# A projection moved by one slot, table loads behind three copies, and sums taken with the copies, in a two-block transformer kernel on one Trainium2 core

## The chip, the cores and the metric

The kernel runs on one core of one Trainium2 chip (trn2). The metric is the device time of one execution in microseconds (us). The kernel before takes 1443.23 us (median of three runs, 1443.16 to 1444.81). Arithmetic is fp32; the large products are split into a rounded high part and a low part (fp32r), three matmuls for one.

## The reference, cut to what matters

Two blocks of two layers each, on 256 tokens of width 1024. The change touches the attention of the first block only. In each of its layers:

```python
h = rms_norm(x, ln1_gain[l]); proj = h @ w_in[l]
o_nsa = nsa_mixer(...)        # 6 heads, selected, window and compressed branches
o_mla = mla_mixer(...)        # 5 heads
o_ret = retention_mixer(...)  # 5 heads; per head: mean and variance over 64 columns, then
                              # (o - mu) * rsqrt(var + eps) * gain, times silu(gate)
x = x + concatenate([o_nsa, o_mla, o_ret]) @ w_out[l]
x = x + square(relu(rms_norm(x, ln2_gain[l]) @ w_up[l])) @ w_down[l]
```

The rotary tables (cos and sin of position times rate) are computed once, at the start of layer 0.

## The kernel before, in words

Every weight passes through a stream. SyncE loads tiles of 1 MB into a ring of four places (`load`, L782). A tile holds two units. ScalarE rounds a unit to its high half `wH` (`feed`, L1522, L1533) once the unit four before it has been used, VectorE subtracts to get the low half `wL` (`feed`, L1973, L1978), and TensorE takes units in order (`next_unit`, L855, which waits for `lo_ready`). Each `project` (L922) is eight chunks of three matmuls into one of four banks in PSUM. Banks are given in the order in which `order1` (L272) names the products; `open_acc` (L841) waits until the bank's last content is drained. So every engine's queue is an order written by hand, and they meet at semaphores.

**Start of layer 0.** TensorE projects cq0, cq1, ckv (units 0 to 2), sums squares (`ss1`), projects q0 (unit 3, in cq0's bank), ks and q1, with the rotation of q0 in the middle of ks and that of ks in the middle of q1 (L1303 to L1305), then `latent_squares` (L1163), which opens the bank that VectorE drains when it reads the rotation of q0 (L2128), then the tokens' projections tm00 and tm01. ScalarE, after four high halves, does `sines` (L1564: waits for VectorE's angles, one Sin over 128x512, signals `trig_ready`), `warm_root` (L1542: one element, so that the root's table is loaded again), copies cq0, cq1, ckv from PSUM (L1613), feeds units 4 to 6, takes the root of ss1 (L1513), and copies q0, ks and q1 (L1617) with a unit behind each. SyncE, after the fifth tile, waits for `trig_ready`, issues 16 small copies of the tables (L819), and only then the sixth tile's load. VectorE does the angles, unit 3's low half, units 4 to 6, the root's refinement, unit 7, waits for the first four table copies (L2269), scales the table (L2188) and rotates q0 and ks.

**Attention.** 17 heads run in 19 slots. In slot i TensorE does one projection of the list `FILL1`, the scores of head i, the transposes of the weights of head i-1 (`weights_transposed`, L1061, which waits for ScalarE's exponentials, L1572 and L1574), the values of head i-2 (`values`, L1069), and small products listed in `END1` (L237): ro0 to ro4 (retention outputs) in slots 13 to 15, mt0 and mt1 (transposes of the mixed output) in slot 16, mt2 in slot 17. The list has 16 names, so slot 16 has a head but no projection; tm31, the last, is in slot 15, beside head 15. In slot 17 TensorE also does 5 filler products (`kept_busy`, L967), and behind mt2 begins the output projection: `side_by_side` (L881) waits for the three units of wo0, wo1, wo2 (units 24 to 26), opens three banks, does two fillers, and then chunk by chunk for the three. Units 24 and 25 are split in slot 14; unit 26 takes the place of a unit of tm31. ScalarE splits it at the end of slot 15 (L1732) and VectorE in slot 16 (L2504), ahead of the low halves of mt0 and mt1 (`mixed_low`, L1987).

**Retention outputs.** ScalarE copies each from PSUM (L1694), 128x128 (two token tiles of 64 columns). VectorE sums them (`group_centred`, L2425), subtracts the mean, squares and sums (`group_squares`, L2432), in slots 15 to 17. It adds one to the gate's tanh and multiplies (`group_gate_open`, L2439) in slot 15 and multiplies by the gain (`group_gate`, L2443) in slot 17. `output` (L2295) scales a head's values and needs TensorE's values of that head.

Of the kernel before, what the change touches and what calls it, by code (L numbers as in the profile page):

```python
# [18 lines left out]
TT = S // P  # L19
# [209 lines left out]
    return out  # L229


FILL1 = ["tm10", "tm11", "q2", "kc", "kw", "vc", "kpe", "rqa", "rka", "rqb", "rkb", "r4", "tm20", "tm21", "tm30", "tm31"]
SLOTS1 = NH1 + 2
MID1 = {3: ["q2"], 4: ["kc"], 5: ["kw"], 7: ["kpe"], 8: ["rqa"], 9: ["rka", "mq0"], 10: ["rqb", "mq1"],
        11: ["rkb", "mq2"], 12: ["r4", "mq3"], 13: ["mq4"]}
# [225 lines left out]
def trn_kernel(nc, consts, vec1, vec2, once, pos, xin, stream, out):  # L461
    ctx = ExitStack()
    with ctx:
# [367 lines left out]
        def _(pe):  # L831
# [48 lines left out]

            def side_by_side(names, y):  # L881

                parts = [blocks(next_unit()) for _ in names]
                banks = [open_acc(n) for n in names]

                def chunk(c):

                    for (wh, wl), a in zip(parts, banks):
                        last = split_product(a[:, 0:S], (wh[:, c, :], wl[:, c, :]), y(c), c == 0, c == KC - 1)
                        if c == KC - 1:  # L890
                            last.then_inc(acc_full, 1)

                return chunk
# [543 lines left out]
        def _(act):  # L1437
# [153 lines left out]
            for L in range(LAYERS):  # L1591
# [14 lines left out]
                            cs = slice(n - 1, n + 1) if n < KC - 2 else slice(n, n + 1)  # L1606
                            act.activation(sq[:, cs, :], x[:, cs, :], ACT.Square).then_inc(sq_ready, 1)
                feed(SPLIT)
                if L == 0:
                    sines()  # L1610
                    warm_root()
                for i, u in enumerate(UNITS1[:SIDE]):
                    take(A1, u, L, raw[:, RAW1[u], :])  # L1613
                feed(SIDE + SPLIT)
                plain_root("ss1", L)
                for i, u in enumerate(("q0", "ks", "q1")):
                    take(A1, u, L, raw[:, RAW1[u], :])  # L1617
                    feed(SIDE + SPLIT + i + 1)
                    if i == 0:
                        for j, v in enumerate(UNITS1[:SIDE]):  # L1620
                            act.wait_ge(acc_drained[A1.bank(v)], A1.drained(v, L))
                            act.activation(latsq3[:, j, :], raw[:, RAW1[v], :], ACT.Square).then_inc(latsq, 1)
# [46 lines left out]
                def taken_after(i):  # L1669

                    for name in END1.get(i, []):
                        n = int(name[-1]) if name[-1].isdigit() else None
                        if name[:3] == "hid":
                            take(A1, name, L, quarters[name == "hidv"], n=P)
                        elif name[:2] == "hs":
                            a = full(A1, name, L)
                            act.activation(gel[:, 0, 30 * (name == "hsv"):30 * (name == "hsv") + 30]
                                           .rearrange("p (g n) -> p g n", g=2),
                                           a[:, 0:32].rearrange("p (g n) -> p g n", g=2)[:, :, 0:N_CMP], ACT.Copy)\
                                .then_inc(acc_drained[A1.bank(name)], 1)  # L1680
                        elif name[:2] == "mq":
                            take(A1, name, L, qm[:, n, :])
                        elif name[:2] == "mk":
                            a = full(A1, name, L)
                            for h in range(n, min(n + 2, MLA_HEADS)):
                                last = act.activation(km[0:64, h, :], a[64 * (h - n):64 * (h - n) + 64, 0:S], ACT.Copy)
                            last.then_inc(acc_drained[A1.bank(name)], 1)
                        elif name[:2] == "mv":
                            take(A1, name, L, vm[:, n, :], n=320)
                        elif name == "ct":  # L1690
                            take(A1, name, L, pcT[0:96, :], rows=slice(0, 96))
                        elif name[:2] == "ro":
                            a = full(A1, name, L)
                            act.activation(ro_(n), a[:, 0:2 * HD].rearrange("p (t d) -> p t d", t=TT), ACT.Copy)\  # L1694
                                .then_inc(acc_drained[A1.bank(name)], 1)
                        elif name[:2] == "mt":
                            mixed_high(n)

# [9 lines left out]
                for i in range(SLOTS1):  # L1708
                    if i < NH1 - 1:
                        feed(fed_by(i))  # L1710
                    if fill1(i):
                        taken(fill1(i))
                    if (L, i) == (0, 1):
                        act.wait_ge(late_in, 16 * 3)
                        act.activation(ada_t, cb2, ACT.Tanh, scale=0.5).then_inc(ctanh, 1)
                    if 1 <= i <= NH1:
                        transposed_copy(i - 1, NH1, 0, L)
                    if i in (NH1 - 2, NH1 - 1):
                        exponentials(i, NH1, 0, L)
                    taken_after(i)  # L1720
                    if i == 8:

                        act.wait_ge(ge, L * 2 + 1)
                        act.activation(gel[:, 1, 0:60], gel[:, 1, 0:60], ACT.Exp, scale=-2.0 * GELU_C).then_inc(ge, 1)
                    if i == 12:

                        act.wait_ge(csub, L + 1)
                        act.activation(pc[:], pc[:], ACT.Exp).then_inc(cexp, 1)
                    if i < NH1 - 2:
                        exponentials(i, NH1, 0, L)  # L1730
                    if i == NH1 - 2:
                        feed(24 + SIDE)  # L1732
                    if i == NH1:
                        warm_root()

                        act.wait_ge(gn_v, L * 2 + 2)
                        act.activation(gnst[:, 3, :], gnst[:, 2, :], ROOT).then_inc(gn_y, 1)
# [170 lines left out]
        def _(dve):  # L1908
# [248 lines left out]
            for L in range(LAYERS):  # L2157
# [263 lines left out]
                def group_centred(first, end):  # L2421

                    o, _, st = group_views(first, end)
                    dve.wait_ge(acc_drained[A1.bank(f"ro{end - 1}")], A1.drained(f"ro{end - 1}", L))
                    link(nc.vector.tensor_reduce(st(0), o, AX.X, ALU.add))  # L2425
                    link(TSC(st(1), st(0), 1.0 / HD, None, ALU.mult))
                    link(TTN(o, o, st(1).unsqueeze(3).to_broadcast([P, TT, end - first, HD]), ALU.subtract))

# [24 lines left out]
                for i in range(SLOTS1):  # L2453
# [21 lines left out]
                        group_centred(3, RET_HEADS)  # L2475
                    if i >= 2:
                        output(i - 2)
                    if i == 15:
                        group_gate_open()
                    if i == 5:  # L2480
                        take_normed("vc")
                    if i == 6:
# [17 lines left out]
                    if i == 14:  # L2500
                        add_compressed()
                        decay_scores(4)
                    if i == 16:
                        feed(24 + SIDE)  # L2504
                    if i == 17:
                        dve.wait_ge(o_drained, L * NH1 + (NH1 - 1) + 1)
                        dve.sem_inc(mla_ready, 1)
# [1 line left out]
                    for name in END1.get(i, []):  # L2509
                        if name[:2] == "mt":  # L2510
                            mixed_low(int(name[2]))
                    if i == 17:
                        group_gate()
                    if i == SLOTS1 - 1:
                        for c in range(IN_TURN, HEADS_DONE):
# [467 lines left out]
```

## Time and profile before

| | |
|---|---|
| median of three runs | 1443.23 us |
| the profiled execution | 1442.89 us, span 1441.1 us |
| TensorE matmuls busy | 1425.9 us, 99% |
| TensorE weight loads busy | 1357.9 us, 94% |
| VectorE busy | 1127.3 us, 78% |
| ScalarE busy | 812.7 us, 56% |
| granted TensorE clock | 1.0 of full speed |
| first block's layer 0, attention | about 12 to 149 us |
| the same of layer 1 | about 331 us later |

Spans and starts are counted from the first instruction; the execution's own time is a little longer than the span. PE is TensorE's matmul, DVE is VectorE, ACT is ScalarE, SPq is the queue of SyncE that issues DMAs. In a timeline a row is: start, duration, engine, line, operation, out<-in, count, and in brackets the idle time of the engine before it with what ended it.

### The profile page before, as it was taken

The numbers are of one execution on the slowest core, as the hardware profiler recorded it, in microseconds if no ns is written. First come the engines' busy times: TensorE is split into PE (matmuls) and PEld (weight loads), VectorE is DVE, ScalarE is ACT, GpSimd is POOL, SyncE is SP. The second block draws the span as 40 slices with busy tenths as digits, with TensorE's granted clock in tenths as the row PEclk, the third lists the DMA queues.
The fourth block names the chain that finished last, engine by engine and source line by source line (L and its number), as shares of the span: only waits on it lengthen the run. The fifth ranks groups of instructions, "written<-read, shape, count | busy, mean of one in ns | idle before, by whom it ended". The sixth has DMA issues, their size and how long they took to land.

```text
span 1441.1 us, 27501 instructions
## 1 busy us (share of the span) xinstructions
PE 1425.9 (99%) x11122; PEld 1357.9 (94%) x11122; DVE 1127.3 (78%) x2045; ACT 812.7 (56%) x1470; POOL 87.4 (6%) x108
## 2 busy tenths in 40 slices
PE   8999999999999999999999999999999999999999
PEld 8989999889989999989999999999899999999998
DVE  6888788896888788897897688777679857876654
ACT  6575677434575587544646456545465554664442
POOL 0000000000000000000150220000005103000000
PEclk9999999999999999999999999999999999999999
DMA  8433488985334379986455454676544445445451
GB/s 286 168 141 123 149 319 315 351 312 220 118 118 176 132 255 333 346 338 237 166 184 181 178 184 164 222 266 252 199 162 168 176 147 184 168 176 205 176 203 61
DMA packets 44445, 297.43 MB, mean 206 GB/s; under 512 B 6048, under 2 KB 7200, under 8 KB 8992
## 3 DMA queue, kind: packets, MB, share of 16 engines
q1 hardware_dynamic: 42880, 295.13, 56.3%
q8 instruction: 89, 1.46, 0.4%
q0 software_dynamic: 1024, 0.53, 0.2%
q14 instruction: 36, 0.29, 0.1%
q10 hardware_dynamic: 416, 0.02, 0.0%
HBM read 293.56 MB, written 1.05 MB: 204 GB/s over the span
## 4 chain that ended last, share of the span: by engine, by line
PE 82%; DVE 12%; ACT 4%; issue 2%; DMA 0%; SPq 0%; DVEq 0%; ACTq 0%
PE acc L864 19%; PE acc L866 18%; PE acc L865 18%; PE acc L870 12%; PE acc L871 6%; DVE wL L1978 5%; ACT wH L1533 2%; PE ps_t L1066 1%; PE ps_s L1053 1%; PE ps_s L1051 1%; PE acc L1156 1%; DVE region L2622 1%; DVE hL L1992 0%; DMA x<-xin 0%; DVE tcs L2619 0%
## 5 line engine op out<-in xcount | busy, mean ns | idle before, releaser
L1978 DVE TENSOR_TENSOR wL<-ring,wH 128x1024 fp32r<-128x1024 f32 x444 | 550.6, 1247 | 218.8 <-ACT wH L1533 210.5
L864 PE MATMUL acc<-hH,wH 128*128 128x256 f32 (+1 forms) x2016 | 577.3, 286 | 6.6 <-ACT region L1460 2.6
L1533 ACT ACTIVATE wH<-ring 128x1024 fp32r<-128x1024 f32 x444 | 464.4, 1052 | 197.2 <-PE acc L871 73.9
L866 PE MATMUL acc<-hH,wL 128*128 128x256 f32 (+1 forms) x2016 | 568.4, 282 | 0.0
L865 PE MATMUL acc<-hL,wH 128*128 128x256 f32 (+1 forms) x2016 | 566.5, 281 | 0.0
L864 PEld LDWEIGHTS acc<-hH,wH 128*128 128x128 f32 x2016 | 379.7, 188 | 13.3 <-issue 5.3
L865 PEld LDWEIGHTS acc<-hL,wH 128*128 128x128 f32 x2016 | 380.8, 189 | 2.0 <-issue 1.4
L866 PEld LDWEIGHTS acc<-hH,wL 128*128 128x128 f32 x2016 | 381.0, 189 | 0.0
L870 PE MATMUL acc<-aHL,wH 128*128 128x512 f32 x448 | 156.7, 394 | 0.0
L871 PE MATMUL acc<-aHL,wL 128*128 128x256 f32 x448 | 124.3, 282 | 0.0
L1968 DVE SCALAR_TENSOR_TENSOR ring<-ring,onc 128x1024 f32<-128x1024 f32 x96 | 117.0, 1219 | 0.0
L870 PE MATMUL acc<-a2HL,wH 128*128 128x512 f32 x308 | 107.3, 393 | 0.0
L870 PEld LDWEIGHTS acc<-aHL,wH 128*128 128x128 f32 x448 | 83.3, 188 | 18.3
L1460 ACT ACTIVATE region<-acc 128x256 f32<-128x256 f32 (+3 forms) x114 | 42.8, 379 | 82.2 <-PE acc L866 78.2
L871 PEld LDWEIGHTS acc<-aHL,wL 128*128 128x128 f32 x448 | 84.2, 188 | 1.2
L871 PE MATMUL acc<-a2HL,wL 128*128 128x256 f32 x308 | 84.8, 283 | 0.0
L870 PEld LDWEIGHTS acc<-a2HL,wH 128*128 128x128 f32 x308 | 57.0, 188 | 12.2
L871 PEld LDWEIGHTS acc<-a2HL,wL 128*128 128x128 f32 x308 | 57.9, 188 | 1.1
L864 PE MATMUL acc<-wH,hH 128*128 128x256 f32 (+1 forms) x192 | 56.4, 294 | 0.1
L865 PE MATMUL acc<-wL,hH 128*128 128x256 f32 (+1 forms) x192 | 53.8, 280 | 0.0
L866 PE MATMUL acc<-wH,hL 128*128 128x256 f32 (+1 forms) x192 | 53.7, 280 | 0.0
L2817 POOL DMA_DIRECT2D weights<-region x32 | 16.8, 531 | 559.1 <-DVE region L2612 559.1
(398 smaller groups left out, 2274.3 us busy)
## 6 DMA issues: line engine op xcount, KB each, us to landing
ring<-stream SPq DMA_DIRECT2D x275, 1024.0 KB, 4.9
cst<-consts SPq DMA_DIRECT2D x1, 1363.0 KB, 14.9
x<-xin SPq DMA_DIRECT2D x4, 256.0 KB, 5.3
ring<-stream SPq DMA_DIRECT2D x2, 512.0 KB, 6.7
out<-x SPq DMA_DIRECT2D x3, 256.0 KB, 5.9
onc<-once SPq DMA_DIRECT2D x1, 516.0 KB, 15.5
weights<-region POOLq DMA_DIRECT2D x32, 16.0 KB, 1.8
v1all<-vec SPq DMA_DIRECT2D x1, 355.0 KB, 8.8
```

The costliest lines, as they stand in the source:

```text
L864: pe.matmul(out, w[0], y[0], start=first, stop=False)
L865: pe.matmul(out, w[0], y[1], start=False, stop=False)
L866: return pe.matmul(out, w[1], y[0], start=False, stop=last)
L870: high = lambda stop: pe.matmul(a[:, :], w[0], both, start=first, stop=stop)
L871: low = lambda: pe.matmul(a[:, 0:S], w[1], both[:, 0:S], start=False, stop=False)
L1051: pe.matmul(b[:, 0:P], q[:, 0:P], k[:, 0:P], start=True, stop=True)
L1053: pe.matmul(b[:, P:3 * P], q[:, P:S], k, start=True, stop=True).then_inc(s_full, 1)
L1460: act.activation(dst, a[rows, 0:n], func, **kw).then_inc(acc_drained[tn.bank(name)], 1)
L1533: act.activation(wH[:, n % SPLIT, :], ring[:, g % RING, half * UNIT:(half + 1) * UNIT], ACT.Copy)\
L1968: STT(products, products, 1.0, cb2, ALU.mult, ALU.mult, accum_out=adac[:, L, 2 * j + half:2 * j + half + 1])\
L1978: TTN(wL[:, n % SPLIT, :], ring[:, g % RING, half * UNIT:(half + 1) * UNIT], wH[:, n % SPLIT, :].bitcast(F32), ALU.subtract).then_inc(lo_r ...
L2817: pool.dma_start(swapped[b % 2][to:to + 8], qk2[row:row + 8, 2 * b:2 * b + 2, :]).then_inc(swapped_in[b % 2], 16)
```

## The change

Six edits, all in the first block's attention:

- `FILL1` gets an empty place ahead of tm31, so tm31 is projected in slot 16 and slot 15 has no projection. The order of the products and their banks follow from it: ro4 comes ahead of tm31.
- `side_by_side` waits for each unit right before its first chunk, not for all three ahead.
- At the start of layer 0 ScalarE's `sines` and `warm_root` stand behind the copies of cq0, cq1, ckv, units 4 to 6 and the root of ss1.
- ScalarE copies a retention output as two instructions of 64 columns, each with its sum (`accum_out`), and VectorE's reduction is left out.
- Unit 26 is split by ScalarE at the end of slot 16 and by VectorE in slot 17, behind mt2's low half.
- `group_gate_open` moves on VectorE from slot 15 to slot 17, behind unit 26.

```diff
-FILL1 = ["tm10", "tm11", "q2", ..., "tm20", "tm21", "tm30", "tm31"]
+FILL1 = ["tm10", "tm11", "q2", ..., "tm20", "tm21", "tm30", None, "tm31"]
...
             def side_by_side(names, y):
 
-                parts = [blocks(next_unit()) for _ in names]
+                parts = []
                 banks = [open_acc(n) for n in names]
 
                 def chunk(c):
 
-                    for (wh, wl), a in zip(parts, banks):
+                    for i, a in enumerate(banks):
+                        if c == 0:
+                            parts.append(blocks(next_unit()))
+                        wh, wl = parts[i]
...
                 feed(SPLIT)
-                if L == 0:
-                    sines()
-                    warm_root()
                 for i, u in enumerate(UNITS1[:SIDE]):
                     take(A1, u, L, raw[:, RAW1[u], :])
                 feed(SIDE + SPLIT)
                 plain_root("ss1", L)
+                if L == 0:
+                    sines()
+                    warm_root()
                 for i, u in enumerate(("q0", "ks", "q1")):
...
                         elif name[:2] == "ro":
                             a = full(A1, name, L)
-                            act.activation(ro_(n), a[:, 0:2 * HD].rearrange("p (t d) -> p t d", t=TT), ACT.Copy)\
-                                .then_inc(acc_drained[A1.bank(name)], 1)
+                            for t in range(TT):
+                                at = t * RET_HEADS + n
+                                last = act.activation(ro_(n)[:, t, :], a[:, HD * t:HD * t + HD], ACT.Copy,
+                                                      accum_out=gnst[:, 0, at:at + 1])
+                            last.then_inc(acc_drained[A1.bank(name)], 1)
...
-                    if i == NH1 - 2:
-                        feed(24 + SIDE)
+                    if i >= NH1 - 2:
+                        feed(24 + min(i - NH1 + 4, SIDE))
...
                     dve.wait_ge(acc_drained[A1.bank(f"ro{end - 1}")], A1.drained(f"ro{end - 1}", L))
-                    link(nc.vector.tensor_reduce(st(0), o, AX.X, ALU.add))
...
-                    if i == 15:
-                        group_gate_open()
...
-                    if i == 16:
-                        feed(24 + SIDE)
...
                     for name in END1.get(i, []):
                         if name[:2] == "mt":
                             mixed_low(int(name[2]))
+                    if i == 16:
+                        feed(24 + 2)
                     if i == 17:
+                        feed(24 + SIDE)
+                        group_gate_open()
                         group_gate()
```

## Rows read from the trace of the kernel before

**Rows 1.** The page, its first part: busy time, share of the span, instructions.
```profile
PE 1425.9 (99%) x11122; PEld 1357.9 (94%) x11122; DVE 1127.3 (78%) x2045; ACT 812.7 (56%) x1470; POOL 87.4 (6%) x108
```

**Rows 2.** Waits of TensorE, whole run: us in total, times, longest us.
```profile
PE ps_s L970 <- DVE mtL L1987: 1.2, 2, 0.6
```

**Rows 3.** Timeline of ScalarE, start of layer 0.
```profile
21.58 0.63 ACT L1567 ACTIVATE region<-region 128x512 f32<-128x512 f32 x1 [4.04 <-DVE region L1955]
22.23 1.28 ACT L1544 ACT_TABLE_LOAD   x1
...
23.76 0.94 ACT L1460 ACTIVATE region<-acc 128x256 f32<-128x256 f32 x3
24.57 2.96 ACT L1533 ACTIVATE wH<-ring 128x1024 fp32r<-128x1024 f32 x3
...
27.68 0.40 ACT L1460 ACTIVATE region<-acc 128x256 f32<-128x256 f32 x1
...
42.29 2.00 ACT L1533 ACTIVATE wH<-ring 128x1024 fp32r<-128x1024 f32 x2
```

**Rows 4.** Timeline of VectorE, start of layer 0.
```profile
21.58 1.23 DVE L1978 TENSOR_TENSOR wL<-ring,wH 128x1024 fp32r<-128x1024 f32 x1
...
32.59 0.68 DVE L2188 TENSOR_TENSOR trig<-trig,rn 128x512 f32<-128x512 f32 x1
...
33.65 0.42 DVE L2128 TENSOR_TENSOR tss<-acc,trig 128x256 f32<-128x256 f32 x1
```

**Rows 5.** Timeline of TensorE, start of layer 0.
```profile
20.67 0.38 PE L977 MATMUL acc<-weights,one 128*128 128x256 f32 x1
...
24.29 0.36 PE L864 MATMUL acc<-hH,wH 128*128 128x256 f32 x1 [2.59 <-ACT region L1460]
...
28.63 0.38 PE L1035 MATMUL acc<-region,cst 128*128 128x256 f32 x1
...
34.21 0.45 PE L1163 MATMUL acc<-weights,one 128*128 128x256 f32 x1 [0.28 <-DVE tss L2128]
```

**Rows 6.** SyncE's table copies; a load at 33.4 to 33.6, and small transfers (us to landing).
```profile
22.30 11.13 SPq L819 DMA_DIRECT2D trig<-region  x16
...
ring<-stream SPq DMA_DIRECT2D x1, 1024.0 KB, 4.8
...
weights<-region POOLq DMA_DIRECT2D x32, 16.0 KB, 1.8
```

**Rows 7.** Timeline of ScalarE, end of slot 14 of layer 0.
```profile
127.22 0.28 ACT L1694 ACTIVATE region<-acc 128x128 f32<-128x128 f32 x1 [0.39 <-PE acc L1252]
127.39 0.39 ACT L1572 ACTIVATE weights<-weights,nmax 128x128 f32<-128x128 f32 x1
...
128.18 0.19 ACT L1574 ACTIVATION_READ_ACCUMULATOR weights<-weights,nmax 128x1 f32 x1
```

**Rows 8.** Timeline of TensorE, slot 15 of layer 0.
```profile
127.96 0.34 PE L864 MATMUL acc<-wH,hH 128*128 128x146 f32 x1
...
130.70 0.43 PE L1051 MATMUL ps_s<-region 96*128 96x128 f32 x2
...
131.40 0.39 PE L1066 MATMUL ps_t<-cst,weights 128*128 128x128 f32 x2
```

**Rows 9.** Timeline of TensorE, slot 17 of layer 0.
```profile
136.95 0.39 PE L1076 MATMUL ps_o<-region,weights 128*128 128x64 f32 x2
...
138.17 0.68 PE L970 MATMUL ps_s<-one 128*128 128x128 f32 x4 [0.61 <-DVE mtL L1987]
...
139.40 0.28 PE L864 MATMUL acc<-mtH,wH 128*128 128x256 f32 x1
```

**Rows 10.** Timeline of VectorE, slots 16 and 17 of layer 0.
```profile
136.14 1.22 DVE L1978 TENSOR_TENSOR wL<-ring,wH 128x1024 fp32r<-128x1024 f32 x1
...
138.13 0.29 DVE L2305 TENSOR_TENSOR region<-ps_o,coef 128x128 f32<-128x128 f32 x1
...
139.56 0.42 DVE L1987 TENSOR_TENSOR mtL<-acc,mtH 128x256 fp32r<-128x256 f32 x1
```

More of the change, by code:

```diff
@@ L229, in down_steps @@
     return out
-FILL1 = ["tm10", "tm11", "q2", "kc", "kw", "vc", "kpe", "rqa", "rka", "rqb", "rkb", "r4", "tm20", "tm21", "tm30", "tm31"]
+FILL1 = ["tm10", "tm11", "q2", "kc", "kw", "vc", "kpe", "rqa", "rka", "rqb", "rkb", "r4", "tm20", "tm21", "tm30", None, "tm31"]
 SLOTS1 = NH1 + 2
```

## The prediction

> **What bounds the kernel.** I read the page first: TensorE is busy for 1425.9 of 1441.1 us [rows 1], so only what stands in TensorE's way counts, and a change that takes nothing away from TensorE can give back its idle time and no more. Then the waits: the changed places hold one wait of 2.59 us at the start [rows 5] and one of 0.6 us at the end of the attention, twice, once a layer [rows 2]. The rest was read engine by engine in the timeline round those two places. The kernel has an order written by hand in each queue, so each part is followed as "who is ready when", in times of the old trace.
>
> **Part 1, the start (layer 0 only).** Before: ScalarE loads the sine's table, idles 4.04 us until VectorE has the angles, does the sine at 21.58, loads the root's table at 22.23, and only then copies cq0, cq1, ckv, from 23.76 [rows 3]. TensorE is done with the sum of squares by 21.5 and wants cq0's bank for q0; it starts at 24.29 [rows 5]. The change puts the three copies first. They no longer hold q0, but q0 needs its own low half, whose subtraction VectorE starts at 21.58 and ends at 22.81 [rows 4], and nothing in VectorE's order changes. So q0 starts at 22.86, 1.43 us earlier, not 2.59.
> What is late next: the transform of q0 in the middle of ks needs ScalarE's copy of q0, which now stands behind the sine. ckv's last product runs just ahead of the sum of squares at 20.67 [rows 5], so its copy starts at about 20.85 and the next instruction at 21.14. Three units and the root of ss1 take 27.68 - 24.57 = 3.11 us [rows 3]: 24.25. Then the first table load, hidden in those idle 4.04 us before and on the path now, 1.28; the sine to the next load 22.23 - 21.58 = 0.65; second load and warm-up 23.76 - 22.23 = 1.53 [rows 3]. The copy of q0 starts at 27.71, where it started at 27.68 before. From such a copy to TensorE's next instruction it was 24.29 - 23.76 = 0.53, so the transform comes at 28.24 instead of 28.63 [rows 5]: TensorE reaches it at 27.2 and waits 1 us. Of 1.43 there remain **0.39 us**.
> The chip needs no longer for a table than the row shows. The Trainium skill, "ScalarE: Activation LUTs", section "What ACT_TABLE_LOAD costs", wants more: 1283 ns for the load and some 1380 ns of drain, 2.66 us for every switch. Its 1283 ns stand in the trace, the drain does not; what the sum would be by it is a rival below.
> The next wait of TensorE is 0.28 us at 34.21, for VectorE's reading of the transform of q0, which began at 33.65 [rows 4, 5]. It needs the first table's copies. Their condition, the sine's end, moves from 22.21 to 24.25 + 1.28 + 0.63 = 26.16. SyncE issues 16 of them in 11.13 us, 0.7 each [rows 6], so the fourth is out at 28.95 and, at 1.8 us to landing for 16 KB [rows 6], there at 30.8. VectorE, whose root and unit 7 come over 2 us earlier, starts the scaling then instead of at 32.59 [rows 4], and the 0.28 us go too. Start: **-0.67 us**; bounds, from the two rows just used: -1.71 (no new wait) and +0.5 (the copies land 3 us later than so).
> Queued behind those copies on SyncE are the loads of weights. The next left at 33.4 and now leaves at 26.25 + 11.13 = 37.4; at 4.8 us [rows 6] its tile is there at 42.2. ScalarE began to split it at 42.29 in the old trace [rows 3], behind tm01. So nothing is lost, with half a microsecond of room: a rival.
>
> **Part 2, tm31 one slot later, and the unit of wo2.** No instruction of TensorE goes or comes; both layers alike. Before: in slot 17 TensorE waits until 138.17, as wo2's bank waits for mt1's low half, and VectorE makes that behind unit 26's low half, begun at 136.14 [rows 9, 10]. The wait costs its 0.61 of idle time and 0.16 more, since two matmuls that take 0.28 each start 0.11 apart (two in 0.39) [rows 9]: 0.77. After: VectorE makes mt0's and mt1's low halves first, at slot 16, so the banks are free; wo0 and wo1 take their first chunk while unit 26 is still open. So far that is a gain.
> But unit 26 now stands in VectorE's slot 17, behind output(15), three instructions of squares and mt2's low half. output(15) needs TensorE's values(15), whose last pair ends at 136.95 + 0.39 = 137.34 [rows 9]. From the start of output(15)'s product at 138.13 to mt2's low half it is 139.56 - 138.13 = 1.43, then 0.42, then the unit's 1.22 [rows 10]: 3.07, and with some 0.08 for two semaphores, wo2's first product can start 3.15 us after values(15). In the old trace it started at 139.40 [rows 9], 2.06 after. Nothing else for TensorE lies between: mt2, two fillers and the two chunks of wo0 and wo1 end about 1.9 us too early. So the old wait goes and a longer one takes its place: **+1.09 us a layer**. Bounds: +0.3, if half of the squares overlapped the wait, and +1.3, if unit 26's high half is late too.
> ScalarE makes that high half after slot 16's exponentials (tm31 must be done first) by about 137.5, before VectorE asks; it delays the copy of head 16's weights to 137.9, which TensorE wants only after 142. group_gate_open (0.8 us, as its like) now stands behind unit 26 as well: VectorE has then the two gate products and a reciprocal, under 2 us, while TensorE does 0.4 + 1.1 + 0.6 us until output(16) can read. It is covered; were the cover gone it would cost its 0.8. Everything behind follows one to one: TensorE waits for VectorE there as before, and is the bound again after it.
>
> **Part 3, slot 15 without a projection.** tm31 ran from 127.96 to 130.70 between the scores and the weights of head 14. The transposes of head 14 now follow the scores of head 15 directly: at 127.96 + (131.40 - 130.70) = 128.66 [rows 8]. Head 14's exponentials end at 128.18 + 0.19 = 128.37 [rows 7]: just in time.
>
> **Part 4, sums with the copies.** VectorE loses a reduction of some 0.5 us in slots 15 and 16. It then waits for TensorE anyway: worth nothing. ScalarE pays: a copy of 128 columns lets the next one start after 127.39 - 127.22 = 0.17 [rows 7]. Two copies of 64 columns with a sum each are not in the trace. Lower bound: nothing more. Upper: an accumulating exponential of 128 columns holds the engine for all of its 0.39, so two such, less 0.17, are +0.6. I take +0.28, nearest the copy's own duration (0.28) less a little, twice. ro2's lies in idle time; ro3's is right ahead of head 14's exponentials: 128.65, and at about 0.25 from ScalarE to TensorE 128.9 against 128.66. **+0.24 us a layer**, 0 to 0.55.
>
> **Sum.** 2 x (1.09 + 0.24) - 0.67 = +2.0 us. The profiled execution took 1442.89 us, 0.34 under the median of 1443.23; so 1444.9 against its own time, and 1445.2 as a median. A measurement of this kernel can tell about 0.2%, 2.9 us, from no change: the forecast is inside.
>
> **Rivals.**
> The wait goes and none takes its place (0.15). For it: the waits named in rows 2 and 5 are the two that the edit addresses. Against: VectorE's order. Price: 2 x 0.77 and 0.67 to 1.71 at the start, -2.2 to -3.2: 1440.0 to 1441.0. It decides if unit 26's low half ends before TensorE has done wo0 and wo1, 1.4 us after values(15).
> Balance (0.16): the start keeps its 1.43, or the squares are hidden; +1.09 a layer shrinks to 0.3 to 0.8. About 1443.2, within 1.
> Slower: the weights behind the tables (0.08). Against it: nothing but the last copies shares the queue with this load, as before, when it took 4.8 us [rows 6]. Landing after 42.8, TensorE waits as long as it is later, as slot 0's scores stand behind these two units on VectorE; it decides at 43.6, from where the total passes 1446.1. At 45.5: 1447.9.
> Slower still by the drain (0.01): twice 1.38 more ahead of q0's copy, the transform at 31.0, 1448.3. Against it speaks the old trace: from the second load to the copy of cq0 it is 1.53 in all [rows 3], with the load's 1.28 and a warm-up in it. That is the rule of the page named above; by the row, it is out.
>
> **Chances.** Forecast 0.60, its own range 1442.5 to 1446.8. Slower by over 0.2% (above 1446.1): 0.13 of the forecast's, and the last two rivals, 0.22. Faster (below 1440.3): 0.12, of the first rival 0.09, and the forecast's far tail. The rest, 0.66, is within. The range from 1440.5 to 1447.3 leaves out the last two rivals and half of the first.
>
> **What would show it.** At the start q0 at 22.9, TensorE waiting about 1 us in ks for ScalarE, the table copies from 26.2 and the next load at 37.4. In the tail the wait before the fillers gone, and a wait of about 1.9 us before the third product of wo's first chunk, by VectorE's subtraction of weights, in both layers; no such wait, or one under 0.8, makes the forecast wrong. ScalarE's retention copies x20 with reads of the accumulator, and a short wait before head 14's transposes.

## The result, and the profile after

| | before | changed |
|---|---|---|
| median | 1443.24 us, 14 runs | 1445.61 us, 14 runs |
| lowest to highest | 1443.07 to 1444.81 | 1443.74 to 1449.30 |
| profiled execution, span | 1442.89, 1441.1 us | 1445.42, 1443.6 us |
| granted clock, mean | 1.000 | 0.999 |

The ratio is 1.0017, with a 95% interval from 1.0010 to 1.0024: slower by 2.4 us, within the 0.2% that count as no change, and 0.4 us from the forecast of 1445.2. Before anything is explained, look at the spread: 5.6 us against 1.7. (Part of that is chance: three larger sets of runs of the kernel before, below, spread over 3.4 to 3.7 us, and a second set of the changed kernel over 4.0.) And the mean clock has lost 0.001.

Part 1 of the page of the changed kernel, against [rows 1]: TensorE is busy for 1.5 us more, though no instruction of it came or went. VectorE is busy for 3.5 us less, of which the four reductions that are gone (0.41 to 0.55 us each) make 1.9, and ScalarE for 1.3 more, with 30 more instructions.

```profile
PE 1427.4 (99%) x11122; PEld 1359.1 (94%) x11122; DVE 1123.8 (78%) x2041; ACT 814.0 (56%) x1500; POOL 87.3 (6%) x108
```

TensorE's waits in the changed kernel (us in total, times, the longest):

```profile
PE acc L864 <- DVE wL L1984: 6.1, 7, 1.8
PE acc L1038 <- ACT region L1463: 0.9, 1, 0.9
```

The wait ahead of the fillers [rows 2] is not in the list any more. The first row read 1.8 in 5 waits before. New in it are the waits for VectorE's low half of weights at q0 (1.2) and at wo2 in each layer (1.8). The second row is the new wait in ks.

**The start.** TensorE's timeline of the changed kernel:

```profile
22.19 0.39 PE L864 MATMUL acc<-hH,wH 128*128 128x256 f32 x1 [1.18 <-DVE wL L1984]
...
27.61 0.70 PE L1038 MATMUL acc<-region,cst 128*128 128x256 f32 x2 [0.89 <-ACT region L1463]
...
32.86 0.60 PE L1166 MATMUL acc<-weights,one 128*128 128x256 f32 x2
```

Its first product of all came 0.69 us sooner than in the execution before (11.04 against 11.73), as its first weights had landed sooner; in another execution of the kernel before it starts at 12.00, so this is no part of the change. Taken off, q0 is 2.10 - 0.69 = 1.41 us earlier than in [rows 5], and latent_squares 1.35 - 0.69 = 0.66.

A better mark than the first product is the start of VectorE's low half of unit 3. It comes right behind the angles that the sine waits for. So in both kernels it moves with what q0 waits for, the copies behind the sine before and that low half now:

```profile
20.91 4.63 DVE L1984 TENSOR_TENSOR wL<-ring,wH 128x1024 fp32r<-128x1024 f32 x4
```

From its start q0 took 24.29 - 21.58 = 2.71 us [rows 4, 5] and takes 22.19 - 20.91 = 1.28; latent_squares took 12.63 and takes 11.95. That is 1.43 and 0.68 us sooner, and it repeats within 0.01 in all five traces that have the sine behind the root. The mark itself lies anywhere from 20.86 to 22.21 us in the fourteen traces, whatever the kernel: this alone moves an execution by up to 1.35 us.

The queue that decides between the two is ScalarE's:

```profile
23.31 0.37 ACT L1516 ACTIVATE rn<-acc 128x256 f32<-128x256 f32 x1
23.70 1.28 ACT L1570 ACT_TABLE_LOAD   x1
25.00 0.63 ACT L1570 ACTIVATE region<-region 128x512 f32<-128x512 f32 x1
25.65 1.28 ACT L1547 ACT_TABLE_LOAD   x1
26.94 0.20 ACT L1547 ACTIVATE warm<-one 128x1 f32<-128x1 f32 x1
27.18 0.38 ACT L1463 ACTIVATE region<-acc 128x256 f32<-128x256 f32 x1
```

The sine and its tables take 27.18 - 23.70 = 3.48 us, all of it between the root and the copy of q0 that TensorE waits for. Each load is followed by the next instruction within 0.02 us: no drain stands behind it.

**The tail.** TensorE and VectorE of the changed kernel, slots 16 and 17 of layer 0, against [rows 9, 10]:

```profile
135.74 0.61 PE L973 MATMUL ps_s<-one 128*128 128x128 f32 x4
136.11 0.36 PE L864 MATMUL acc<-mtH,wH 128*128 128x256 f32 x1
...
138.82 0.39 PE L864 MATMUL acc<-mtH,wH 128*128 128x256 f32 x1 [1.76 <-DVE wL L1984]
```

```profile
135.79 0.29 DVE L2311 TENSOR_TENSOR region<-ps_o,coef 128x128 f32<-128x128 f32 x1 [0.62 <-PE ps_o L1079]
136.23 0.42 DVE L2437 TENSOR_TENSOR region<-region 128x256 f32<-128x256 f32 x1
136.69 0.42 DVE L2438 TENSOR_REDUCE region<-region 128x4 f32<-128x256 f32 x1
137.14 0.17 DVE L2439 TENSOR_SCALAR region<-region 128x4 f32<-128x4 f32 x1
137.22 0.42 DVE L1993 TENSOR_TENSOR mtL<-acc,mtH 128x256 fp32r<-128x256 f32 x1
137.55 1.22 DVE L1984 TENSOR_TENSOR wL<-ring,wH 128x1024 fp32r<-128x1024 f32 x1
```

VectorE's rows are the queue that the prediction walked: output(15), three instructions of squares, mt2's low half, and only then unit 26. wo2's first product waits for its end. From the last product before to it TensorE loses 138.82 - 136.78 - 0.11 = 1.93 us (136.78 is the start of that product, 0.11 the usual spacing); in layer 1 it is 1.94. Where the execution had stood 1.66 us ahead of the one before, it stands 0.58 ahead: +1.08, and +1.06 in layer 1.

**The clock.** Windows of the changed kernel around wo's first chunk in layer 1 (us, then busy time of PE, PEld, DVE, ACT, POOL, each with its count; then granted clock, DMA share, GB/s):

```profile
470.00:472.80 2.80, 1.03 (x9) 0.85 (x8) 2.73 (x6) 1.17 (x3) 0.00 (x0) 1.00 0.00 0
472.80:476.30 3.50, 3.50 (x20) 3.50 (x19) 1.20 (x4) 0.42 (x2) 0.00 (x0) 0.51 0.02 5
476.30:480.00 3.70, 3.70 (x32) 3.53 (x32) 2.87 (x7) 1.37 (x3) 0.00 (x0) 1.00 0.00 0
```

TensorE waits 1.94 us, runs from 471.95, and at 472.8 its granted clock drops to half, 1.2 in place of 2.4 GHz, for 3.41 us. In 3.5 us it does 20 matmuls; the kernel before does 33 in the same window:

```profile
472.80:476.30 3.50, 3.50 (x33) 3.50 (x32) 2.74 (x8) 1.61 (x3) 0.00 (x0) 1.00 0.00 0
```

The execution's lag behind the one before grows by 1.5 us there. Nothing in the prediction speaks of it.

The bridge of the two spans, from starts of the same matmuls: inputs -0.7, start -0.7, slot 0 -0.3, tail +1.1, behind it +0.1, two small steps of +0.2 and +0.4 near 263 and 288 us, tail of layer 1 +1.1, clock +1.5, the rest -0.1: +2.5, as 1443.6 - 1441.1. The 0.3 of slot 0 is a gain that the prediction did not name: in the kernel before, TensorE's transposes of head 0 start at 48.65, 0.32 us behind the product ahead of them in place of 0.12, and 0.25 behind the end of ScalarE's exponentials. In the changed kernel nothing holds them.

### The profile page after: what moved, and what is told of

The parts are those of the page before. It is cut to its first block, busy times and chain, and to the rows that moved or that the text cites. A ratio compares the mean times of both kernels' runs of the same rounds, so it can differ in the third digit from the quotient of the medians.

```text
span 1443.6 us, 27525 instructions
## 1 busy us (share of the span) xinstructions
PE 1427.4 (99%) x11122; PEld 1359.1 (94%) x11122; DVE 1123.8 (78%) x2041; ACT 814.0 (56%) x1500; POOL 87.3 (6%) x108
## 3 DMA queue, kind: packets, MB, share of 16 engines
HBM read 293.56 MB, written 1.05 MB: 204 GB/s over the span
## 4 chain that ended last, share of the span: by engine, by line
PE 76%; DVE 14%; ACT 5%; DMA 3%; issue 1%; DVEq 0%; POOL 0%; ACTq 0%; POOLq 0%
PE acc L864 17%; PE acc L866 17%; PE acc L865 17%; PE acc L870 11%; DVE wL L1984 6%; PE acc L871 6%; DMA ring<-stream 3%; ACT wH L1536 2%; DVE ring L1974 1%; PE ps_t L1069 1%; PE ps_s L1056 1%; PE ps_s L1054 1%; PE ps_t L973 1%; PE acc L1159 1%; PE ps_o L1079 1%
## 5 line engine op out<-in xcount | busy, mean ns | idle before, releaser
L870 PE MATMUL acc<-aHL,wH 128*128 128x512 f32 x448 | 156.9, 394 | 0.1
L870 PE MATMUL acc<-a2HL,wH 128*128 128x512 f32 x308 | 107.3, 393 | 0.0
L870 PEld LDWEIGHTS acc<-aHL,wH 128*128 128x128 f32 x448 | 83.3, 188 | 18.9 <-DVE wL L1984 0.7
L870 PEld LDWEIGHTS acc<-a2HL,wH 128*128 128x128 f32 x308 | 57.0, 188 | 12.2
```

Source lines behind the costliest of these rows:

```text
L870: high = lambda stop: pe.matmul(a[:, :], w[0], both, start=first, stop=stop)
```

## The experiments

All were compared with runs of the kernel before on the same chip, whose medians were 1443.22 (25 runs), 1443.20 (33) and 1443.33 (27) in the three batches. Line numbers shift by a few between kernels.

### The change taken apart

**The kernel before once more**, for its trace.

> The kernel before, once more, for a second trace of it. Both theories: 1443.1 to 1443.6 us, clock at its upper level all the way. It shows how far the first inputs' landing (7.67 us for the first weights in the old trace, 7.22 in the changed kernel's) moves by itself: if that is chance, a start between 11.0 and 11.8 us for the first product is seen here too.

1443.46 us. Windows around the start's wait:

```profile
20.00:24.40 4.40, 1.98 (x14) 1.55 (x13) 2.46 (x5) 2.97 (x7) 0.00 (x0) 1.00 0.98 399
24.40:28.00 3.60, 3.60 (x20) 3.60 (x19) 2.47 (x3) 3.19 (x5) 0.00 (x0) 0.53 0.90 310
```

The kernel before loses its clock too, here after the start's wait: I had expected full clock all the way, a miss. The first trace of it had not lost it (31 matmuls in the window where this has 20). Whether it happens thus changes from execution to execution. As one fall of 3.41 us takes 0.0012 off the mean clock, every run's mean clock tells about how many it had: 1.000 none, 0.999 one, less than that more than one. Of the 25 runs of the kernel before beside this one, 9 show 1.000 (median 1442.68) and 16 show 0.999 (1443.28). The changed kernel's 14 runs: four at 1.000 (median 1444.19), six at 0.999 (1445.61), two at 0.998 (1448.17), two at 0.997 (1446.99). The order of the last two shows how rough medians of so few runs are.

**Only the sine moved**, on the kernel before:

```diff
                 feed(SPLIT)
-                if L == 0:
-                    sines()
-                    warm_root()
...
                 plain_root("ss1", L)
+                if L == 0:
+                    sines()
+                    warm_root()
```

> The kernel before with the sine moved behind the three copies, and nothing else. Theory A (the start gives back 0.67 us, and the spread of the changed kernel's runs comes from the wait for unit 26 in the tail, through TensorE's clock): 1442.5 us, all runs within 1 us, the wait of 2.59 us gone, 1.43 at q0 and about 1.05 in ks in its place. Theory B (the weights' loads, pushed back behind the table copies, come late over the whole layer, and that is the spread): a spread of 2 us or more already here, median 1443.5 or above.

1442.62 us (1441.84 to 1444.12), ratio 0.9996 (0.9987 to 1.0005), all 11 runs at clock 1.000. In its trace the wait at q0 and the one in ks are those of the changed kernel (1.44 and 1.06 us between starts), and latent_squares comes 0.68 us sooner, counted from VectorE's unit 3. The medians do not show that gain: the runs of the kernel before beside it have 1442.68 at full clock, 0.06 more, so what its median gains (0.6 us against 1443.22) is no more than the falls of the clock that are gone. The trace shows one way in which the rest is lost: at 619 us TensorE waits 0.5 us for VectorE's low half of a unit, whose tile ScalarE had waited for until 618.34.

**Only the tail**: the changed kernel with `sines` and `warm_root` back ahead of the copies.

> The changed kernel with the sine back in its old place: the tail alone. Theory A: 2 x 1.05 us for the wait, 1445.3 where the clock holds, and up to 1.7 us more for each layer in which it halves after the wait, so a spread of 2 us or more and a median of 1445.5 to 1447. Theory B: 1445.3 with all runs within 1 us, as the table copies are where they were.

1446.98 us (1445.99 to 1448.28), ratio 1.0026 (1.0016 to 1.0036). No run of 9 has clock 1.000; they stand at 0.999 to 0.997. Its trace shows the clock halved twice, after the start's wait and after the tail's in layer 1:

```profile
24.10:27.50 3.40, 3.01 (x14) 3.04 (x15) 1.56 (x2) 3.40 (x6) 0.00 (x0) 0.52 0.93 337
470.40:474.40 4.00, 2.24 (x19) 2.04 (x19) 3.39 (x7) 2.59 (x6) 0.00 (x0) 1.00 0.00 0
474.40:477.90 3.50, 3.50 (x21) 3.50 (x19) 1.39 (x4) 0.05 (x1) 0.00 (x0) 0.52 0.02 5
```

Against the kernel before it is 3.8 us slower. Two waits of 1.09 more explain 2.2, and the fall in layer 1 takes 1.6 in its trace (the lag grows from 3.0 to 4.6 us). That trace also has a wait of 0.6 us near 600 us, of the kind that `start_only` has at 619, so the split of the rest is rough.

**The changed kernel with work in the tail's wait**: eight filler products ahead of wo2's unit. The wait's end is set by VectorE and stays.

```diff
                         if c == 0:
+                            if i == SIDE - 1:
+                                kept_busy(8, ps_s[1])
                             parts.append(blocks(next_unit()))
```

> The changed kernel with 8 filler products (16 matmul passes, about 1.8 us) on TensorE just before it waits for unit 26. They lie inside the wait, so they cost nothing by themselves. Theory A: the clock stays at its upper level in every run, 1443.24 - 0.67 + 2.1 = 1444.7 us, all runs within 1 us. Theory B, or if the wait alone costs: no change against the changed kernel's 1445.6, with its spread of 1443.7 to 1449.3.

1444.14 us (1443.54 to 1446.03), ratio 1.0007 (0.9998 to 1.0015), all 11 runs at 1.000. TensorE is held up as long as before, but busy, and it is 1.5 us faster than the changed kernel's 1445.61 and equal to that kernel's own runs at full clock, 1444.19. In its trace the tail still costs 1.07 and 1.06 us against the kernel before, as without the fillers. So the 1.5 us are the clock's and follow from the idle wait.

**The same at the start of the kernel before**: eleven fillers between ss1 and q0.

> The kernel before with 11 filler products (22 passes, 2.4 us) on TensorE inside its wait of 2.59 us at the start. They end before q0 could start, so nothing is added to the path. Theory A (the wait halves TensorE's clock for 3.4 us in most runs of the kernel before, and that costs 0.6 to 1.1 us): every run at the full clock, median 1442.6 against 1443.2. Theory B (the clock is no cause): 1443.2 as before.

1442.88 us (1442.08 to 1446.63), ratio 0.9998 (0.9989 to 1.0007), all 11 runs at 1.000, where 21 of the 33 runs beside it were below. Those 33 have a median of 1442.82 at 1.000 and of 1443.33 at 0.999: a fall there costs 0.5 us (0.6 and 0.8 in the other two batches). The traces show where the rest goes, counted from VectorE's unit 3: with the fall, latent_squares comes 1.08 us later (13.71 in place of 12.63, in three traces against two), and head 0's transposes only 0.82 later (27.87 in place of 27.06), as TensorE waits there for ScalarE in the kernel before.

**Unit 26 early**: the changed kernel, with VectorE's half of unit 26 back in slot 16, behind the low halves of mt0 and mt1. `group_gate_open` stays in slot 17.

```diff
                     if i == 16:
-                        feed(24 + 2)
+                        feed(24 + SIDE)
                     if i == 17:
-                        feed(24 + SIDE)
                         group_gate_open()
```

> The changed kernel with one thing put back: VectorE makes unit 26's low half in slot 16, now behind the low halves of mt0 and mt1, and not in slot 17 behind the squares. Theory A (the tail's wait is VectorE's order, 1.05 us a layer and the halved clock behind it): the wait of 1.8 us before wo2's first product is gone, the clock at its upper level in all runs, 2 x (1.9 to 2.3) us less what VectorE is then late with output(16), about 0.5: a median of 1442.0 to 1443.0. Theory C (tm31's new place itself costs, as slot 15 has no cover): no wait at wo2, but one of 0.5 us or more in slots 15 and 16, and 1443.5 or above.

1442.86 us (1441.68 to 1444.88), ratio 0.9997 (0.9988 to 1.0006), all 10 runs at 1.000. The wait at wo2 is gone. In its place stand 0.76 us (between starts) before a later chunk of wo, for VectorE's mtL, and 0.39 before the transpose behind it, in both layers. TensorE's waits:

```profile
PE acc L864 <- DVE mtL L1993: 2.2, 4, 0.6
```

This row was 1.0 in 2 waits in the changed kernel. Of 1.93 us of waiting a layer 1.15 are left: the queue of VectorE is full, and moving one piece out of the way moves the wait on. Against the changed kernel it gains 2.75 us, 1.3 at full clock (1444.19 less 1442.86).

**The changed kernel again**, in the last batch.

> The changed kernel once more, for the share of runs with a halved clock beside runs of the kernel before on the same chip. Theory A: where the mean clock is 1.000 it takes 1444.2, as fill_wait does; 0.7 to 1.7 us more for each halving (0.0012 of mean clock); median 1445 to 1446.

1446.00 us (1443.71 to 1447.72), ratio 1.0015 (1.0006 to 1.0024); four runs at 1.000 have a median of 1444.84, five at 0.999 of 1446.36. At full clock that is 0.6 us over the 1444.2 that I expected. The profiled execution again shows 1.93 us at wo2 in both layers and half the clock from 474.8 us on, for 3.41 us. It also has a wait that the first trace had not:

```profile
PE ps_t L1069 <- ACT weights L1577: 1.0, 1, 1.0
```

That is head 0's transposes, and the cause lies upstream, in SyncE's queue and then ScalarE's:

```profile
26.39 12.29 SPq L819 DMA_DIRECT2D trig<-region  x16
38.72 8.62 SPq L787 DMA_DIRECT2D ring<-stream  x5
```

```profile
43.54 2.01 ACT L1536 ACTIVATE wH<-ring 128x1024 fp32r<-128x1024 f32 x2 [1.90 <-DMA ring<-stream]
```

The table's 16 copies took 12.29 us to issue; in the first trace of the changed kernel they took 11.13:

```profile
25.72 11.13 SPq L819 DMA_DIRECT2D trig<-region  x16
36.89 2.08 SPq L787 DMA_DIRECT2D ring<-stream  x4
```

```profile
41.71 2.01 ACT L1536 ACTIVATE wH<-ring 128x1024 fp32r<-128x1024 f32 x2 [0.74 <-DMA ring<-stream]
```

So ScalarE got the tile behind them at 43.54 in place of 41.71, 4.8 us after its issue in both, and TensorE paid for it. This is the rival of the late weights, which the prediction gave 0.08: of five traces with the sine moved behind the root (both of the changed kernel, the sine alone, the fillers, unit 26 early) two have this wait, 0.98 and 0.64 us. They are the two in which the copies took longer than 11.13 us to issue, 12.29 and 11.93. And there is no room: from ScalarE's start on the tile to head 0's transposes it is 5.28 or 5.29 us in four of the five traces, with and without a wait in the list, and 5.32 in the first trace of the changed kernel.

### Sums with ScalarE's copies, alone

The kernel before, with the 64-column copies and without VectorE's reduction.

> The kernel before with the sums taken by ScalarE's copies alone. All theories: 1443.2, same within 0.3. ScalarE's retention copies are 20, with 20 reads of the accumulator, and each head holds ScalarE 0.2 us longer; VectorE's two reductions a layer are gone and it waits for TensorE instead.

1442.24 us (1441.51 to 1442.99), ratio 0.9991 (0.9982 to 1.0000), six of 10 runs at 0.999: a miss, 1.0 us under what I expected. The waits say where it comes from:

```profile
PE ps_s L970 <- DVE mtL L1990: 0.3, 2, 0.2
```

In the kernel before this row reads 1.2 in 2 waits [rows 2]. VectorE's slots 16 and 17 of this kernel, against [rows 10]:

```profile
134.83 0.17 DVE L2428 TENSOR_SCALAR region<-region 128x4 f32<-128x4 f32 x1
135.03 0.43 DVE L2429 TENSOR_TENSOR region<-region 128x256 f32<-128x256 f32 x1
135.49 0.17 DVE L2301 RECIPROCAL coef<-psumv 128x2 f32<-128x2 f32 x1
135.69 0.29 DVE L2308 TENSOR_TENSOR region<-ps_o,coef 128x128 f32<-128x128 f32 x1
135.90 1.22 DVE L1981 TENSOR_TENSOR wL<-ring,wH 128x1024 fp32r<-128x1024 f32 x1
137.03 0.75 DVE L1990 TENSOR_TENSOR mtL<-acc,mtH 128x256 fp32r<-128x256 f32 x2
```

Nothing waits in that row of instructions up to mt1's low half, which holds TensorE. In the kernel before a reduction of 0.41 us stands ahead of the first of them. Without it all come 0.45 us sooner against the scores before, in both layers, which is the 0.9 us. ScalarE's price is nil: in the changed kernel, too, its copies of ro2 and ro3 do not hold TensorE up.

```profile
125.56 0.22 ACT L1699 ACTIVATE region<-acc 128x64 f32<-128x64 f32 x1 [0.15 <-PE acc L1255]
125.68 0.19 ACT L1699 ACTIVATION_READ_ACCUMULATOR region<-acc 128x1 f32 x1
125.77 0.21 ACT L1699 ACTIVATE region<-acc 128x64 f32<-128x64 f32 x1
125.88 0.20 ACT L1699 ACTIVATION_READ_ACCUMULATOR region<-acc 128x1 f32 x1
125.97 0.40 ACT L1575 ACTIVATE weights<-weights,nmax 128x128 f32<-128x128 f32 x1
```

A head takes 125.97 - 125.56 = 0.41 us, each instruction starting before the one ahead ends. Head 14's exponentials and TensorE's transposes of them:

```profile
126.75 0.19 ACT L1577 ACTIVATION_READ_ACCUMULATOR weights<-weights,nmax 128x1 f32 x1
```

```profile
126.62 0.60 PE L1056 MATMUL ps_s<-region 96*128 96x256 f32 x2
127.06 0.49 PE L1069 MATMUL ps_t<-cst,weights 128*128 128x128 f32 x3
```

The exponentials end at 126.94 and the transposes start at 127.06, 0.44 us behind the scores' last two products, as in the kernel before (130.96 to 131.40): no gap.

### Versions that keep the gain

**The tail in the better order**, on the kernel before: units one by one in `side_by_side`, and unit 26 behind the low halves of mt0 and mt1, but still in slot 16.

```diff
-                    if i == 16:
-                        feed(24 + SIDE)
...
                             mixed_low(int(name[2]))
+                    if i == 16:
+                        feed(24 + SIDE)
```

> The kernel before with two edits: TensorE waits for each of wo's units only before its first chunk, and VectorE's unit 26 stands in slot 16 behind the low halves of mt0 and mt1 instead of ahead of them. tm31, the sine and the sums stay. Theory A: the wait of 0.77 us before the fillers goes in both layers and none comes: -1.5 us, 1441.7 (the start's wait of 2.59 us and its halved clock in most runs remain). Theory C (the gain needs tm31 in slot 16): the wait moves to wo2's first product, 1443.2.

1441.88 us (1440.24 to 1444.17), ratio 0.9991 (0.9982 to 1.0000). The waits of [rows 2] are gone in both layers and none takes their place; the start's wait is left, and with it six of 11 runs at 0.999. Median against median it is 1.3 us, for two waits of 0.77. Here the runs with the fall are not the slower ones (median 1441.84, against 1442.60 of the five at full clock), so the price of a fall at the start is not to be read from sets this small.

**The start split**, on the kernel before: copies of cq0 and cq1 and unit 4 ahead of the sine, ckv's copy and the rest behind it.

```diff
-                if L == 0:
-                    sines()
-                    warm_root()
                 for i, u in enumerate(UNITS1[:SIDE]):
+                    if i == SIDE - 1 and L == 0:
+                        feed(1 + SPLIT)
+                        sines()
+                        warm_root()
                     take(A1, u, L, raw[:, RAW1[u], :])
```

> The kernel before with the start in a third order: copies of cq0 and cq1 and unit 4 ahead of the sine, ckv's copy behind it. The first table load is hidden in ScalarE's idle time again, q0's copy comes early, and the table copies and the loads behind them leave as before. Theory A (what q0's copy waits for is the table load and the sine): no wait in ks, -1.7 us at the start, and no halved clock: 1441.3 to 1441.7 against start_only's 1442.6. Rival: another wait takes its place (unit 4's or 5's low half), 1442.5.

1441.10 us (1440.50 to 1443.24), ratio 0.9983 (0.9974 to 0.9992), all 11 runs at 1.000. In TensorE's timeline q0 waits less and the transform in ks not at all:

```profile
22.41 0.39 PE L864 MATMUL acc<-hH,wH 128*128 128x256 f32 x1 [0.95 <-DVE wL L1979]
...
26.79 0.59 PE L1035 MATMUL acc<-region,cst 128*128 128x256 f32 x2
```

The sine is done in the time that ScalarE would spend idle (19.83 to 23.27 in its trace), and both copies that TensorE waits for are in time. Counted from VectorE's unit 3, latent_squares comes 12.63 - 10.88 = 1.75 us sooner than in the kernel before, and the medians at full clock differ by 1442.82 - 1441.10 = 1.72. So the bound that I had given for "no new wait", -1.71 at the start, can be had, with another order.

**Both together.**

> swap_tail and split_start together, on the kernel before: tm31 and the sums stay as they were. Theory A (the two waits are independent, and both that TensorE has in the changed places can go): 1443.2 - 2.1 - 1.4, 1439.6 to 1439.9 us, clock at its upper level in all runs. If they share a cause: 1441 or above.

1439.24 us (1438.54 to 1441.27), ratio 0.9973 (0.9962 to 0.9984), all 7 runs at 1.000. This beats both kernels: 4.1 us under the kernel before, 6.4 under the changed one. It is 0.4 us under the lower end of what I expected. Whether the sums with the copies would add to it was not tried.

**The change repaired**: tm31 moved and sums with the copies as in the change, the start split, and on VectorE in slot 16 the low halves, `group_gate_open` and unit 26, in this order.

> The changed kernel, kept in tm31's place and the sums, with VectorE's unit 26 in slot 16 behind mt0's, mt1's low halves and group_gate_open, and with the start of split_start. Theory A: no long wait at wo2, VectorE about 0.8 us earlier with output(16) than in unit_early: 1439.8 to 1440.8, so at best level with swap_and_split: the new place of tm31 earns nothing by itself. Theory C (tm31 in slot 16 is worth its move once the unit is right): 1439.3 or below.

1440.11 us (1439.22 to 1442.59), ratio 0.9977 (0.9967 to 0.9987), all 9 runs at 1.000. No better than the plainer one: with the sums and tm31's move on top nothing is gained over the order on VectorE. tm31's move was never run alone.

## Why the prediction was right, and where it was not

**Part 1, the start: right as a chain of waits.** q0 was to come 1.43 us sooner and did, counted from VectorE's unit 3; then a wait of about 1 us in ks (1.05 between starts), then the 0.28 us gone: -0.67 against -0.68 measured, in all five traces. What it is worth in device time is less sure: alone, it left 0.06 us between medians at full clock. The Trainium skill's rule ("ScalarE: Activation LUTs", "What ACT_TABLE_LOAD costs") of some 1380 ns of drain behind the load does not hold here: the sine starts at 25.00 behind a load from 23.70 that takes 1.28.

**The late tile: named, but with too little chance.** I counted the room as half a microsecond and gave 0.08. The room was next to nothing: with the same 11.13 us of issue it is 0.04 in the first trace of the changed kernel, and 1.16 us more of issue cost TensorE 0.98. I had taken the room from ScalarE's start in the old trace, but TensorE waited behind that chain already (the 0.3 of slot 0), and in the changed kernel it gets there 0.67 us sooner. And the issue time was taken as the one value of [rows 6], and it changes from execution to execution, 11.11 to 12.29 us. In two of five traces it shows, at up to 1 us.

**Part 2, the tail: right.** The wait at wo2 was to be about 1.9 us in place of 0.77: it is 1.93 and 1.94. +1.09 a layer was forecast, +1.08 and +1.06 measured. When VectorE's unit 26 moves back to slot 16, the wait at wo2 goes.

**Part 3: right**, head 14's transposes start without a gap.

**Part 4: wrong twice.** "+0.24 us a layer" for ScalarE: it was 0. The price on ScalarE itself was near: I had 0.28 more a head, and it is 0.41 - 0.17 = 0.24. What failed is the step from there to TensorE. I had added 0.25 us between the end of the exponentials and the transposes. That is what the traces show where TensorE stands and waits for them (48.57 to 48.83 in the second trace of the changed kernel); here it was still busy with the scores, and started 0.12 us after the end of the exponentials, without a gap. And "VectorE loses a reduction ... worth nothing": I looked for the wait right behind the reduction. With the order of before nothing stops VectorE between it and mt1's low half, and there it is worth 0.45 us a layer. In the change as it is, this gain isn't seen, as VectorE waits 0.62 us for values(15) ahead of output(15), which stands before unit 26; the error cost the sum nothing, but the explanation was wrong.

**The clock: missing.** The forecast had no term for it. By runs at full clock the median of the changed kernel is at 1444.19, or 1444.84 in the later batch, 1.5 to 2.1 us over the kernel before at full clock, where I had +2.0; the other 1.4 us of its median are the clock's. It is partly offset by the kernel before, whose median also holds some falls (0.4 to 0.6 us over its clean runs). So the forecast of 1445.2 was met within 0.4 us with help: 0.48 too much in Part 4 stood in for a cost I did not know. That the spread would grow I could not say at all; the two highest runs, 1447.5 and 1449.3, lie outside my range.

What stays open: why the two steps near 263 and 288 us. In that stretch ScalarE waits longer for tiles of weights, 54.5 us in 22 waits against 31.5 in 14, with the same traffic, 310 GB/s. Waits of this kind, for a unit's low half in the products of L870, are in seven of the fourteen traces, up to 1.0 us long, and the second trace of the changed kernel has none: they change from execution to execution. Why a tile is late was not tried. Nor was it tried why some waits of 1.9 us halve the clock and others, of the same length, don't: in three traces with that wait (the changed kernel's two and the tail alone) layer 0's kept it and layer 1's lost it.

## What to carry to other kernels

A wait on the bounding engine can cost more than its length. Before an edit trades two short waits for one long, look at the granted clock behind the long ones, in several executions, and put harmless work into those that can't be removed. When work is taken off an engine's queue, follow the queue to the next instruction that somebody waits for, not to the next wait of the engine itself. And when a blocking step (a table load, a burst of small DMA issues) must go somewhere, find the idle time it used to sit in, and move around it only what is urgent: here two copies, not three.

## What the hardware showed that I had not expected

- The granted clock fell to half for 3.41 us behind waits of TensorE: after idle times of 2.2 to 2.6 us at the start (16 of 25 runs of the kernel before are at mean clock 0.999 in one batch, 21 of 33 and 16 of 27 below 1.000 in the others, and one trace with 2.59 kept it), and after 1.93 in the tail (10 of the changed kernel's 14 runs are below 1.000). In all 70 runs of the seven kernels where such waits were filled, shortened or removed the clock stayed at 1.000; the longest unfilled wait in their traces, behind the first product, is 1.45 us between starts.
- The same fall costs 0.5 to 0.8 us at the start (0.82 in the traces by head 0's transposes) and about 1.5 in the tail, where little is given back (the lag goes from 2.8 to 2.6 us).
- A copy of 64 columns with its sum costs ScalarE 0.2 us, the reading of the accumulator (0.19) half hidden behind the next copy; two such cost 0.24 more than one plain copy of 128 columns (0.17 [rows 7]).
- From the end of ScalarE's exponentials to TensorE's transposes it is 0.25 us where TensorE waits for them, and 0.12 was enough where it was still busy with products before.
- Sixteen small copies took SyncE 11.11, 11.13, 11.13, 11.93 and 12.29 us to issue in the five traces with the sine behind the root (12.57 in one with the sine in its old place), and the load of weights behind them in the queue inherits that spread.
